# Gather and result buffers of an expert loop: three and four in place of four and three

## The reference

```
grp_prob = softmax(hf @ w_grp + b_grp);  gp, gi = top_k(grp_prob, 1)
ev, ei = top_k(expert logits of that group, 2)
gates = softmax(ev) * gp, at expert gi * 8 + ei
y = sum over experts of (silu(h @ w_gate) * (h @ w_up) * gate) @ w_down
```

## Time and profile before

| | us |
|---|---|
| median of 3 runs (848.21 to 848.63) | 848.57 |
| the profiled execution, its own time | 845.96 |
| its span | 844.2 |
| TensorE busy | 792.5 |
| VectorE busy | 485.3 |
| GpSimd busy | 280.8 |

### The profile page before, as it was taken

How to read it: one execution, slowest core, us unless ns; L and a number is a source line. 1 busy time by engine, 2 the same in 40 slices (tenths; PEclk the granted TensorE clock), 3 DMA queues, 4 the chain that set the end, 5 groups by cost and what they waited for, 6 DMA issues and landing times.

```text
span 844.2 us, 16685 instructions
## 1 busy us (share of the span) xinstructions
PE 792.5 (94%) x6779; PEld 530.8 (63%) x6779; DVE 485.3 (57%) x1202; ACT 240.8 (29%) x574; POOL 280.8 (33%) x267
## 2 busy tenths in 40 slices
PE   8999999999999999899989999999999999999950
PEld 7556544454444444687877555657988888887830
DVE  3860468888841133778765757566645455554434
ACT  6320021111110030667542222413223222232214
POOL 5820000000199900634661000000345656442332
PEclk9999999999999999999999999999999999999985
DMA  9934444334300120400003725255777999888639
GB/s 323 336 88 141 138 135 132 124 125 159 116 26 27 48 75 1 137 20 4 4 5 138 294 94 196 103 156 203 269 229 224 334 306 272 281 260 290 200 83 364
DMA packets 86964, 136.30 MB, mean 161 GB/s; under 512 B 17293, under 2 KB 59498, under 8 KB 86890
## 3 DMA queue, kind: packets, MB, share of 16 engines
q1 hardware_dynamic: 76586, 118.44, 41.0%
q0 software_dynamic: 10304, 16.82, 8.4%
HBM read 124.18 MB, written 29.92 MB: 183 GB/s over the span
## 4 chain that ended last, share of the span: by engine, by line
PE 78%; DVE 12%; issue 3%; DMA 2%; ACT 2%; SPq 1%; POOL 1%; DVEq 0%; POOLq 0%; ACTq 0%
PE banks L827 73%; PE banks L1556 3%; DVE REG_Y L1931 3%; DVE REG_P L2662 1%; ACT REG_W L1604 1%; PE banks L1449 1%; DMA REG_P<-y_d 1%; DMA prow<-in_conv_w 1%; DVE REG_P L1931 1%; DVE REG_W L2038 1%; ACT REG_P L1604 1%; DVE mx L2041 1%; PE banks L1124 1%; DMA y_d<-REG_W,idx 1%; DVE REG_W L2080 1%
## 5 line engine op out<-in xcount | busy, mean ns | idle before, releaser
L827 PE MATMUL banks<-REG_W 128*128 128x512 f32 (+2 forms) x1144 | 323.5, 448 | 1.4 <-DVE REG_W L2617 1.1
L827 PEld LDWEIGHTS banks<-REG_W 128*128 128x128 f32 (+1 forms) x1144 | 163.2, 184 | 140.0 <-issue 139.3
L827 PE MATMUL banks<-REG_W,REG_Y 128*128 128x128 f32 (+1 forms) x484 | 115.3, 390 | 2.2 <-DVE REG_W L2350 1.9
L827 PEld LDWEIGHTS banks<-REG_W,REG_Y 128*128 128x128 f32 x484 | 67.8, 196 | 32.3 <-issue 30.0
L1604 ACT ACTIVATE REG_P<-banks 128x256 f32<-128x256 f32 (+2 forms) x102 | 46.8, 479 | 127.1 <-PE banks L827 118.6
L827 PE MATMUL banks<-REG_P 64*64 64x64 f32 (+3 forms) x2496 | 72.9, 233 | 8.0 <-issue 3.9
L1604 ACT ACTIVATE REG_W<-banks,mod,s 128x128 f32<-128x128 f32 x136 | 51.2, 457 | 85.8 <-PE banks L1556 85.8
L827 PEld LDWEIGHTS banks<-REG_P 64*64 64x64 f32 (+1 forms) x2496 | 61.7, 135 | 18.1 <-issue 10.1
L668 POOL TENSOR_TENSOR REG_P<-REG_P 128x1040 f32<-128x1040 f32 x2 | 4.8, 2389 | 175.8 <-DVE REG_P L2017 175.8
L1931 DVE SCALAR_TENSOR_TENSOR REG_Y<-REG_P,cc,REG_Y 128x256 f32<-128x256 f32 x112 | 54.3, 485 | 4.0
L764 POOL DMA_INDIRECT y_d<-REG_W,tbl x22 | 34.9, 1589 | 64.0 <-DVE REG_W L2625 64.0
(11 more groups left out here) (317 smaller groups left out, 1150.1 us busy)
## 6 DMA issues: line engine op xcount, KB each, us to landing
REG_P<-in_w_ada SPq DMA_DIRECT2D x20, 1024.0 KB, 6.7
REG_W<-in_w_in SPq DMA_DIRECT2D x17, 512.0 KB
REG_P<-in_moe_w_down SPq DMA_DIRECT2D x17, 512.0 KB, 11.4
REG_P<-in_moe_w_up SPq DMA_DIRECT2D x14, 512.0 KB, 10.3
REG_P<-in_moe_w_gate SPq DMA_DIRECT2D x13, 512.0 KB, 7.8
REG_Y<-in_moe_w_gate SPq DMA_DIRECT2D x11, 512.0 KB, 6.9
REG_W<-in_moe_w_up SPq DMA_DIRECT2D x10, 512.0 KB, 9.6
REG_W<-in_moe_w_down SPq DMA_DIRECT2D x10, 512.0 KB, 18.3
```

The costliest lines, as they stand in the source:

```text
L827: return pe.matmul(o_, l, r, start=start, stop=stop, skip_group_check=True)
```

## The change

Six edits that belong together. There are three gather buffers and four result buffers; the area x1[:, 6] goes from the one kind to the other. At the start gathers of tiles 0 to 2 are issued in place of 0 to 3. In the loop, `gather_behind(e + BUF)` behind the scatter of tile e issues the gather of tile e + 6 where it was e + 7. The overflow's gather into buffer 0 stands behind the scatter of the e with e + BUF = 32, so 29 where it was 28, and waits for the transposes of tile 30, the last own user of buffer 0 (it was tile 28). The counts of landings on buffer 0 follow: `OWN`, the number of tiles 0 to 31 that use it, is 11, where E // BUF was 8.

```diff
@@ -35,8 +35,9 @@
 TURN = [(i % GROUPS) * EPG + i // GROUPS for i in range(E)]
 TILES = E + OVT
 RING = 11
-BUF = 4
-RES = 3
+BUF = 3
+RES = 4
+OWN = len(range(0, E, BUF))
@@ -263,8 +264,8 @@
-        xg = [xg2[:, 0], xg2[:, 1], x1[:, 5], x1[:, 6]]
-        yo = [yo2[:, 0], yo2[:, 1], x1[:, 7]]
+        xg = [xg2[:, 0], xg2[:, 1], x1[:, 5]]
+        yo = [yo2[:, 0], yo2[:, 1], x1[:, 6], x1[:, 7]]
@@ -782,18 +783,18 @@
                     gp.wait_ge(s["m_tx"], e + 1)
                     gather(TURN[e + BUF], e % BUF)
 
-            for e in range(3):
+            for e in range(BUF):
                 gather_behind(e)
             for e in range(E):
                 gp.wait_ge(s["m_yd"], e + 1)
                 scatter_add(rows_of(TURN[e], 0), e % RES)
-                gather_behind(e + 3)
+                gather_behind(e + BUF)
                 if e == E - 1:
                     gp.wait_ge(s["m_tx"], E + 1)
                     gather(E + 1, 0)
                 if e + BUF == E:
                     gp.wait_ge(s["far_ld"], 32)
-                    gp.wait_ge(s["m_tx"], E - BUF + 1)
+                    gp.wait_ge(s["m_tx"], max(range(0, E, BUF)) + 1)
                     gather(E, 0)
@@ -808,7 +809,7 @@
-                gp.wait_ge(s_gx[0], i * 16 + 16 * (E // BUF + 2))
+                gp.wait_ge(s_gx[0], i * 16 + 16 * (OWN + 2))
@@ -1586,7 +1587,7 @@
-            ex_t(E, 0, 16 * (E // BUF + 1))
+            ex_t(E, 0, 16 * (OWN + 1))
@@ -1595,7 +1596,7 @@
-                ex_t(i + (E + 1), 0, i * 16 + 16 * (E // BUF + 2))
+                ex_t(i + (E + 1), 0, i * 16 + 16 * (OWN + 2))
```

## The result

The changed kernel takes 852.98 us (median of 7 runs, 851.69 to 855.99); the kernel before, measured beside it, 848.21 (median of 7, 845.15 to 849.14). The ratio is 1.0061, with a 95% interval of 1.0038 to 1.0084: some 5 us slower. Each experiment was measured beside the kernel before on one chip, in three groups with three chips, where that kernel took 847.39, 847.93 and 847.87 us. Two kernels of different groups are therefore best compared by their ratios: 0.1% is 0.85 us. The profiled execution took 851.69 us with a span of 849.5, against 845.96 and 844.2 before.

The account below looks back on a forecast made before the run. It took TensorE, with 78% of the chain of waits, to bound the kernel, from turn 25 on weight transfer as much. Terms 0 + 0 + 3.6 + 1.3 = 4.9 us gave 853.5 us, range 850.2 to 856.8.

Parts of the forecast that it names:

- Result buffers: Expert loop: results wait for TensorE alone, no scatter delays one, so a fourth result buffer is worth 0.
- Gathers one turn later: Expert loop: each gather is issued a turn later, at least 2.3 us of lead remain, cost 0.
- Weights and the stall in the middle: Turns 26 to 31: weights of turns 26 and 27 land 1.0 us sooner; gain 0.8 to loss 1.0, taken as 0.
- turn 31's weights: Loop's end: they still land at 796.8, so the steady train of turns gains at most 0.8 us.
- rival (b): Middle of the loop: the stall at turn 26 goes and stays away, 849.8 us, no measurable change; chance 0.08.
- The overflow's gather: Loop's end: issued 6.2 us later, landing at 806.7, delaying TensorE by 3.6 us, bounds 2.0 and 6.2.
- Rival (a): Loop's end: the overflow's gather lands in 3.9 us, delay 2.0 us, no clock drop, 850.6 us; chance 0.12.
- the estimate by the Trainium skill's fit: Overflow's gather: 2.0 us plus bytes over 436 GB/s gives 3.2 us, delay 1.3 us, 849.9 us in all.
- The clock behind it: After TensorE's idleness at the loop's end: work partly at 1.2 GHz costs 1.3 us, bounds 0 and 1.7.
- Everything behind moves along, no cover: Loop's end: tile 31's result and scatter, the overflow's products and scatter and the last stage all move by the same amount.

Follow-up runs that it names:

- e1: The changed kernel with the overflow's gather back behind the scatter of tile 28: 848.04 us, ratio 1.0017 to the kernel before.
- e10_buf2: The changed kernel with two gather buffers in place of three, the overflow's gather behind the scatter of tile 30: 954.92 us, ratio 1.1244 to the kernel before.
- e2: The kernel before (four gather, three result buffers) with only the overflow's gather moved behind the scatter of tile 29: 852.06 us, ratio 1.0063 to the kernel before.
- e4: The changed kernel with the overflow's gather directly ahead of the scatter of tile 29: 848.98 us, ratio 1.0019 to the kernel before.
- e8_awake_half: The changed kernel with 16 extra matmuls on TensorE before the overflow's transposes: 851.59 us, ratio 1.0045 to the kernel before.
- e5: The changed kernel with three result buffers in place of four: 854.0 us, ratio 1.0071 to the kernel before.
- e11: The changed kernel with two result buffers in place of four: 853.7 us, ratio 1.0066 to the kernel before.
- e7_down_first: The changed kernel with TensorE's down product of tile 31 ahead of the overflow's transposes: 854.18 us, ratio 1.0078 to the kernel before.
- e6: The changed kernel with the overflow's gather one place later, behind the scatter of tile 30: 858.78 us, ratio 1.0113 to the kernel before.
- e3: The changed kernel with 32 extra matmuls on TensorE before the overflow's transposes: 854.19 us, ratio 1.0080 to the kernel before.

## Why the prediction was right

The forecast was 853.5 us, slower; measured were 852.98. The difference to the kernel before was forecast as 4.9 us and is 4.8 by the medians, 5.2 by the ratio. The terms can be checked one by one; the mechanism is the one foreseen, and some of the closeness is luck, as said at the terms.

**Result buffers, 0.** Right: no wait for a scatter in the list, and the same time with three and with two, as finely as these runs tell.

**Gathers one turn later, 0.** Right by the trace: no wait for a gather between tile 3 and tile 31. By the times e1 bounds it, for all of them together and whatever else the buffers do, at 0 to 2.8 us. That their lead was what made this free, and nearly used up, is what e10_buf2 shows; the forecast of at least 2.3 us left met 2.5 in e1.

**Weights and the stall in the middle, 0 between -0.8 and +1.0.** The trace gives +0.25, less than e2 and the kernel before differ by in the same stretch (1.2 us). The waits came near what was worked out: 0.76 us at turn 26 (0.6 foreseen), 2.06 at turn 27 (1.7 foreseen), and the clock drop set behind the second as the costly case did not come. But e2, with the old buffers, shows the second wait too and no drop either, so this agreement is no proof that a gather fewer moved the weights. One step was wrong: turn 31's weights were to keep their place and the train to gain from that. Counted from tile 0 they came some 0.7 us later than before, the last step of their semaphore at 798.58, and TensorE waited 0.59 us for them. Until then the train had been half a microsecond ahead. The waits were moved, not removed, so rival (b) fell by its own condition.

**The overflow's gather, 3.6.** Measured 3.88 from the products of turn 31, 4.1 from tile 0. The issue came 1.87 us behind the scatter of tile 29, as foreseen, but that scatter came half a microsecond early, with the train: counted from tile 0 the gather is issued 5.7 us later than before, not 6.2. The landing took 6.5 us instead of 5.5. Of the two misses the first takes back half of the second, so the term is closer than its parts; that much is luck. The argument that swapping gather and scatter leaves the end of the pair where it was is borne out by e4: 8.4 us from the pair's first issue in both orders. Rival (a), a landing in 3.9 us, is refuted, and with it the estimate by the Trainium skill's fit (page "DMA: Bandwidth & Descriptors", the section on the anatomy of one DMA on the gpsimd path), which gave 3.2 us: no placement of this gather landed in less than 4.8. That estimate also took too many bytes. The software queue's 16.82 MB in 68 large transfers are 0.25 MB each, not the 0.5 MB of 128 rows of 4 KB: the index lists are filled up with rows that are not there. In the changed kernel that queue moved 0.10 MB from 821 to 826 us, where the overflow's scatter lies, so its tile has some 25 rows. For them the same fit gives an estimate of 2.2 us, further off still.

**The clock behind it, 1.3.** Measured 1.24 in the trace, and the same taken away again by e8_awake_half. That there is such a term is shown; that it met 1.3 so closely is luck of the execution, since the same kind of wait cost 1.2 to 2.7 us in e2, e5 and e11, and 2.7 lies outside the bounds of 0 and 1.7.

**Everything behind moves along, no cover.** Right: from the transposes on, nothing but the clock differs, and e7_down_first shows that the order of the work queued behind them is not what costs.

## What to carry to other kernels

A buffer taken from one use and given to another moves the whole hand-written order along; ask for each moved item not how much slack the typical one has, but which one had none. Here 29 gathers (tiles 3 to 31) had a turn to spare, and the one at the end of the list, whose place hung on the same constant, had none: TensorE already waited 0.24 us for it. It cost the whole difference, as far as these runs tell, and it could have been placed on its own condition (a free buffer and its index list) instead of on that constant.

Where a transfer comes late and TensorE idles for it, reckon the wait and then the slow stretch behind it: a quarter of this loss was the second, and in other traces of such a wait it was up to 2.7 us.

## What was not expected of the hardware

The clock drop is not a plain function of the last wait. The kernel before stood 1.85 us at turn 26 and dropped; the changed kernel stood 2.06 us at turn 27 and did not, e6 2.13 us and did not, e3 2.10 us and did, with 32 matmuls in 5.43 us. In e10 waits of 2.66 and 2.74 us passed without a drop, and waits of 2.83 and 2.85 us did not. From 3.65 us on, a drop came each time, but not always at once: in e5, behind a wait of 3.70 us, the eight transposes still took 1.09 us, and the clock fell to 0.50 behind them, at about 809.8.

The landing of an indirect gather of the same rows ran from 8.1 to 4.8 us within 15 us of the loop's end, depending on when it was issued. A price for it taken from another place in the trace would have been off by up to 3 us.
